# When GpSimd sums the squares of a norm in a three-block transformer kernel: behind the last remainder, or behind the split of the fourth weight tile

## The chip, the cores and the metric

The kernel is one program on one core of a Trainium2 chip. TensorE multiplies, VectorE and ScalarE work on elements, GpSimd adds squares and loads bias tables, SyncE issues the loads of the weights. The metric is the device time of one execution in microseconds, of which lower is better. The kernel before took 1948.46 us (median of three).

## The reference

The input x has 512 tokens of 1024 values. Three blocks follow each other: block A with windowed attention, block B with neighbourhood attention on a grid, and a third with dilated and stick-breaking attention. Each norm divides by a root of a mean of squares over the 1024 values of a token:

```python
def rms_norm(x, g):
    xf = x.astype(jnp.float32)
    y = xf * lax.rsqrt(jnp.mean(xf * xf, axis=-1, keepdims=True) + RMS_EPS)
    return (y * g.astype(jnp.float32)).astype(x.dtype)
```

In blocks A and B (i = 0 and 1) the part that matters here is

```python
        x = x + rms_norm(mixed, norm_mix_post[i])
        h = rms_norm(x, norm_ffn_pre[i])
        gu = jnp.einsum('bsd,df->bsf', h, w_gu[i])
        f = jnp.einsum('bsf,fd->bsd', jax.nn.silu(gu[..., :D_FF]) * gu[..., D_FF:], w_down[i])
        x = x + rms_norm(f, norm_ffn_post[i])
```

and then the next block's norm and its projection to queries, keys and values.

## The kernel before, in words

Activations lie with the feature on the partitions: x is `xT`, eight chunks of 128 features by 512 tokens. Each weight matrix is cut into tiles of 128 output features by 1024 input features. SyncE loads a tile into one of four slots of `w_raw`. ScalarE rounds it to `w_hi` (L566), VectorE subtracts to get the remainder `w_lo` (L982) and counts `w_split`. In the same way the activations are kept as `h_hi` (ScalarE, L609) and `h_lo` (VectorE, L1004, which counts `h_ready`). A product takes three matmuls for each chunk: `w_hi h_hi`, `w_hi h_lo`, `w_lo h_hi` (L1516 to L1518), so 24 matmuls of 512 columns for a tile.

The stages touched here are of the kind "stair": the two `gate_up` stages (44 tiles each), `proj[1]` (14 tiles) and `proj_dil` (12 tiles). Their tiles 0, 1 and 2 are multiplied together, chunk by chunk, as the chunks of the new x come out of the norm before (`stairs`, L1422 to L1430). From tile 3 on each tile is done in a whole. Before each tile TensorE waits for its `w_split`.

The norm that belongs to the stage doesn't hold the matmuls up. The gain is applied to h at once, and the factor for each token, `rstd`, is applied when a product's bank is read. So the mean of squares is made meanwhile: ScalarE squares the eight chunks into `sq_x` (L647), GpSimd adds them (`sum_kept`, L474, seven adds) and splits the sum into `sum_hi` and `sum_lo` (L480, L482), TensorE sums over the partitions with a matrix of minus ones (`add_all`, L1629 and L1630), and ScalarE takes a logarithm and an exponential (`statistic`, L618 and L621). These norms have the numbers 3 and 7 (for `gate_up`), 5 (for `proj[1]`) and 9 (for `proj_dil`).

Where TensorE makes the product over partitions is given by hand: `hooks` maps a place (tile, chunk) of the stage's order to a function that is called behind that chunk's three matmuls. `turn_rms` is a second hook: it waits for `rstd` and turns it into columns with matmuls of one column (L1639, L1641), for values that are read with tokens on the partitions.

The engines keep their own order. VectorE, in `dense`, splits tile k + 3 at step k and then reads the bank of tile k; eight tiles are split in front of step 0, so the first split in this loop is tile 8's, at step 5, behind the reads of tiles 0 to 4. ScalarE does the same with `w_hi`. In `gate_up` the reads (L1193) scale an even tile (gate) and an odd tile (up), ScalarE takes the Silu of the gate (L795), VectorE multiplies (L1198), ScalarE rounds (L798) and VectorE subtracts (L1200).

When GpSimd starts is a wait of its own:

```python
                pool.wait_ge(h_ready, DC * (4, 6)[layer] - 1)
                sum_kept(3 + 4 * layer, sq_x, S)
```

It starts at the seventh of the eight `h_lo` of this norm.

Of the kernel before, what the change touches and what calls it, by code (L numbers as in the profile page):

```python
# [11 lines left out]
DC = D // P  # L12
# [27 lines left out]
def program(nc, t, out):  # L40
# [25 lines left out]
    proj, mem_k, mem_v, v_in, w_out, gate_up, down = [], [], [], [], [], [], []  # L66
# [15 lines left out]
    proj_dil = Stage(tiles_of(t["w_qk_dil"], 12), stair=True)  # L82
# [13 lines left out]
    with ExitStack() as ctx:  # L96
# [76 lines left out]
        rstd = place("rstd", [P, S])  # L173
# [26 lines left out]
        ps = [ctx.enter_context(nc.psum_tensor(f"bank{i}", [P, 512], F32)) for i in range(8)]  # L200
# [6 lines left out]
        w_hi_done, w_split, unit_done = sem("w_hi_done"), sem("w_split"), sem("unit_done")  # L207
# [239 lines left out]
        def _(pool):  # L447
# [87 lines left out]
            for layer in range(2):  # L535
                if layer:
                    pool.dma_start(grid_masks[:, :], t["grid_masks"]).then_inc(masks_in, 16)
                    pool.wait_ge(masks_in, 16)
                biases(layer)
                sum_streamed(2 + 4 * layer)  # L540

                pool.wait_ge(h_ready, DC * (4, 6)[layer] - 1)
                sum_kept(3 + 4 * layer, sq_x, S)
                sum_streamed(4 + 4 * layer)
                pool.wait_ge(h_ready, DC * (5, 7)[layer] - 1)
                sum_kept(5 + 4 * layer, sq_x, S)
            biases(2)
            sum_streamed(10)
# [826 lines left out]
        def _(pe):  # L1375
# [115 lines left out]
            def dense(st, rhs, reads, wait_rhs=lambda chunk: None, hooks={}, begun=()):  # L1491

                begin_side()
                seen = 0
                if st.stair:
                    stairs(st, rhs, wait_rhs)
                for k, i, c in chunk_order(st):
                    if (k, c) in begun:  # L1500
                        continue
                    u, first, m = st.tiles[k][i]
                    if i == 0 and c == 0 and bank_before(st, k) >= 0:
                        s, n = reads(bank_before(st, k))
                        pe.wait_ge(s, n)
                    if c == 0:
                        pe.wait_ge(w_split, u + 1)
                    chunk = first + c
                    if k == 0:
                        wait_rhs(chunk)  # L1510
                    hi, lo = rhs(chunk) if st is not gates or k % 3 == 0 else (o2_hi[:, chunk, :], o2_lo[:, chunk, :])
                    acc = bank_of(st, side[0], k)[:, :st.width]
                    cols = slice(P * c, P * c + P)
                    w1, w2 = w_hi[:, u % 4, cols], w_lo[:, u % 4, cols]
                    start, end = i == 0 and c == 0, i == len(st.tiles[k]) - 1 and c == m - 1
                    mm(acc, w1, hi, start=start, stop=False)  # L1516
                    mm(acc, w1, lo, start=False, stop=False)  # L1517
                    last = mm(acc, w2, hi, start=False, stop=end)  # L1518
                    if c == m - 1:
                        last.then_inc(unit_done, 1)  # L1520
                    if (k, chunk) in hooks:
                        hooks[k, chunk]()
# [18 lines left out]
            def reads_of(sem_, base, counts=None):  # L1541
                return lambda k: (sem_, base + (k + 1 if counts is None else sum(counts[:k + 1])))
# [79 lines left out]
            def add_all(n, acc, width=S):  # L1622

                def add():
                    if n_norm[0]:
                        pe.wait_ge(ln_done, n_norm[0])
                    pe.wait_ge(masks_rounded, 3)
                    pe.wait_ge(sum_split, kept_stats.index(n) + 1)
                    mm(acc[:, :width], neg_ones[:, :], sum_hi[:, :width], start=True, stop=False)  # L1629
                    mm(acc[:, :width], neg_ones[:, :], sum_lo[:, :width], start=False, stop=True).then_inc(sq_summed, 1)  # L1630
                    n_norm[0] += 1
                return add

            def turn_rms(n, src, tiles, acc, first=0, classes=False):

                def turn():
                    pe.wait_ge(rstd_done, n + 1)
                    for r in range(4 if classes else 0):
                        mm(acc[:, 4 + r:5 + r], by_class(src[:, :])[:, r, :], ident[:, 0:1], start=True, stop=True)  # L1639
                    for kt in range(tiles):  # L1640
                        last = mm(acc[:, first + kt:first + kt + 1], src[:, P * kt:P * kt + P], ident[:, 0:1],  # L1641
                                  start=True, stop=True)
                    last.then_inc(col_ready, 1)
                    n_col[0] += 1
                return turn
# [153 lines left out]
            for layer in range(2):  # L1799
                n = 5 * layer  # L1800
                old = 4 * ((side[0] + 1) % 2)
                if layer == 0:
                    n_h[0] += DC

                counts = [1] * 6 + [4] * 2 + [1] * 2 if layer == 0 else [1] * 14

                def turn_both():
                    pe.wait_ge(rstd_done, 2)
                    pe.wait_ge(consts_in, 64)
                    turn_rms(0, rstd, 4, ps[old])()  # L1810
                    turn_rms(1, rstd_mem, 2, ps[old], 8)()

                if layer == 0:
                    hooks = {(3, 0): turn_table, (5, 2): add_first, (8, 3): add_all(1, ps[old], MEM), (9, 3): turn_both}
                else:
                    hooks = {(5, 2): add_all(n, ps[old]), (6, 3): turn_rms(n, rstd, 4, ps[old])}
                dense(proj[layer], h, reads_of(acc_read_dve, n_dve[0], counts), wait_h, hooks)
                end_side(dve=sum(counts), lent=sum(counts[:7]))
                if layer == 0:
                    n_h[0] += DC  # L1820
                    dense(mem_k[0], mh, None, wait_h)
                    end_side(dve=2)
                    values(mem_v[0], mh_hi, mh_lo, 2)
                if layer == 0:
                    values(v_in[0], h_hi, h_lo, 4)
                    n_h[0] += DC
                    dense(mem_k[1], mh, None, wait_h)
                    end_side(dve=2)
                    softmax(0, None, None, None, (mem_v[1][0], mh_hi, mh_lo, 2, 1), w_out[0])
                else:  # L1830
                    values_wide(v_in[1][0], h_hi, h_lo, 2)
                    softmax(1, None, None, None, (v_in[1][1], h_hi, h_lo, 4, 2), w_out[1])
                for inner in range(2):
                    n = 2 + 4 * layer + 2 * inner
                    new, old = 4 * (side[0] % 2), 4 * ((side[0] + 1) % 2)
                    if inner == 0:
                        def wait_o(c):
                            if c == DC - 1:
                                pe.wait_ge(o_ready, heads[0] - DC + c + 1)
                        dense(w_out[layer], h, reads_of(acc_read_act, n_act[0]), wait_o,  # L1840
                              {}, [(k, c) for k in range(2) for c in range(7)] + [(2, 0), (2, 1)])
                    else:
                        dense(down[layer], a, reads_of(acc_read_act, n_act[0]), wait_a(FC))
                    end_side(act=4)
                    after = (gate_up[layer], (proj[1], proj_dil)[layer])[inner].tiles[0][0][0]
                    wait_reads(freed[-2])
                    add_seven(n, ps[old + 3])()
                    add_last(n, ps[old + 3])
                    keep_busy(14, after)
                    n_x[0] += DC  # L1850
                    n_h[0] += DC
                    freed[-1] = (n_act[0], n_dve[0], n_x[0])
                    if inner:
                        continue
                    dense(gate_up[layer], h, reads_of(acc_read_dve, n_dve[0]), wait_h, {(5, 2): add_all(n + 1, ps[new])})
                    n_a[0] += FC
                    end_side(dve=2 * FC, lent=7)

            old = 4 * ((side[0] + 1) % 2)
            counts = [4] * 2 + [1] * 10  # L1860
            dense(proj_dil, h, reads_of(acc_read_dve, n_dve[0], counts), wait_h,
                  {(5, 2): add_all(9, ps[old]), (6, 3): turn_rms(9, rstd, 4, ps[old], 0, True)})
            end_side(dve=18, lent=13)
            values(v_dil[:1], h_hi, h_lo, 4)
            pe.wait_ge(hi_classed, DC)
# [245 lines left out]
```

## Time and profile before

| what | us |
|---|---|
| median of three runs | 1948.46 (1947.61 to 1950.47) |
| profiled execution, its own time | 1947.74 |
| its span, first to last instruction | 1945.9 |
| TensorE busy | 1927.0 |
| VectorE busy | 971.4 |
| ScalarE busy | 774.5 |
| GpSimd busy | 182.4 |

The span is covered by TensorE for 99%. Ends of matmuls are modelled and overlap the next start, so the distance between two starts says more than the duration. The profile names a line, an engine and the tiles written and read.

### The profile page before, as it was taken

What the parts mean: (1) busy time and instruction counts of PE and PEld (TensorE: products, weight loads), DVE (VectorE), ACT (ScalarE), POOL (GpSimd) and SP (SyncE); (2) the same over time, 40 slices, a digit from 0 to 9 for tenths busy, and PEclk for the clock granted to TensorE, in tenths of its full rate; (3) what the DMA queues carried; (4) which work ended last, traced back from release to release, by engine and by line L of the source; (5) the groups of instructions that cost most, each with busy time, mean ns of one, the idle gap of its engine ahead of it and who ended that gap; (6) DMA issues with size and microseconds to landing.
All of it is one profiled execution on the core that took longest, in us unless ns stands there. A gap on an engine that the chain in (4) does not pass through costs nothing.

```text
span 1945.9 us, 24129 instructions
## 1 busy us (share of the span) xinstructions
PE 1927.0 (99%) x9956; PEld 1568.2 (81%) x9956; DVE 971.4 (50%) x1464; ACT 774.5 (40%) x1252; POOL 182.4 (9%) x197
## 2 busy tenths in 40 slices
PE   9999999999999999999999999999999999999997
PEld 7967788888878867788888887878888888888886
DVE  5575665553227366565554227343665556425522
ACT  5386433333423176433333325233764443212321
POOL 4111300000105030210000003000000020000000
PEclk9999999999999999999999999999999999999999
DMA  6421223333333221233333333331212333322322
GB/s 192 142 60 44 86 90 97 96 97 100 92 101 99 94 64 34 80 99 93 97 97 98 94 101 108 98 109 44 77 30 87 111 98 98 98 95 94 96 96 85
DMA packets 52117, 178.72 MB, mean 92 GB/s; under 512 B 6380, under 2 KB 7788, under 8 KB 51880
## 3 DMA queue, kind: packets, MB, share of 16 engines
q1 hardware_dynamic: 49656, 169.14, 27.7%
q0 software_dynamic: 2208, 7.97, 1.5%
q8 instruction: 80, 1.31, 0.3%
q14 instruction: 29, 0.24, 0.0%
q10 hardware_dynamic: 144, 0.06, 0.0%
HBM read 174.48 MB, written 2.66 MB: 91 GB/s over the span
## 4 chain that ended last, share of the span: by engine, by line
PE 96%; DVE 2%; ACT 1%; issue 0%; DMA 0%; SPq 0%; DVEq 0%; ACTq 0%
PE bank L1516 24%; PE bank L1517 23%; PE bank L1518 23%; PE bank L1760 3%; PE bank L1717 2%; PE bank L1682 2%; PE bank L1535 2%; PE bank L1536 2%; PE bank L1537 2%; PE bank L1430 1%; PE bank L1422 1%; PE bank L1425 1%; PE bank L1574 1%; PE bank L1575 1%; PE bank L1576 1%; PE bank L1594 1%
## 5 line engine op out<-in xcount | busy, mean ns | idle before, releaser
L982 DVE TENSOR_TENSOR w_lo<-w_raw,w_hi 128x1024 fp32r<-128x1024 f32 (+2 forms) x325 | 403.9, 1244 | 733.9 <-ACT w_hi L566 733.4
L566 ACT CAST w_hi<-w_raw 128x1024 fp32r<-128x1024 f32 (+2 forms) x325 | 328.5, 1012 | 581.3 <-DMA w_raw<-in_w_down 133.7
L1516 PE MATMUL bank<-h_hi,w_hi 128*128 128x512 f32 x1288 | 503.0, 391 | 0.2 <-DVE q_buf L1048 0.2
L1517 PE MATMUL bank<-h_lo,w_hi 128*128 128x512 f32 x1288 | 501.8, 390 | 0.0
L1518 PE MATMUL bank<-h_hi,w_lo 128*128 128x512 f32 x1288 | 501.8, 390 | 0.0
L1516 PE MATMUL bank<-a_hi,w_hi 128*128 128x512 f32 (+1 forms) x752 | 289.4, 385 | 0.0
L1517 PE MATMUL bank<-a_lo,w_hi 128*128 128x512 f32 (+1 forms) x752 | 289.2, 385 | 0.0
L1518 PE MATMUL bank<-a_hi,w_lo 128*128 128x512 f32 (+1 forms) x752 | 289.1, 384 | 0.0
L1516 PEld LDWEIGHTS bank<-h_hi,w_hi 128*128 128x128 f32 x1288 | 242.0, 188 | 53.4 <-DVE w_lo L982 1.6
L1518 PEld LDWEIGHTS bank<-h_hi,w_lo 128*128 128x128 f32 x1288 | 242.2, 188 | 50.8
L1517 PEld LDWEIGHTS bank<-h_lo,w_hi 128*128 128x128 f32 x1288 | 242.2, 188 | 49.8
L1516 PEld LDWEIGHTS bank<-a_hi,w_hi 128*128 128x128 f32 x752 | 141.3, 188 | 28.3 <-DVE a_lo L1312 0.3
L1518 PEld LDWEIGHTS bank<-a_hi,w_lo 128*128 128x128 f32 x752 | 141.3, 188 | 28.2
L1517 PEld LDWEIGHTS bank<-a_lo,w_hi 128*128 128x128 f32 x752 | 141.3, 188 | 28.1
L460 POOL COPY sq_sum<-sq 128x512 f32<-128x512 f32 x6 | 3.7, 624 | 1061.1 <-ACT sq L605 1061.1
L693 ACT ACTIVATE prob_short<-prob_short,low_stat 128x256 f32<-128x256 f32 (+6 forms) x144 | 74.7, 525 | 19.8 <-DVE low_stat L1093 19.8
L463 POOL TENSOR_TENSOR sq_sum<-sq_sum,sq 128x512 f32<-128x512 f32 x37 | 51.7, 1397 | 283.0 <-ACT sq L605 283.0
L798 ACT CAST a_hi<-raw 128x512 fp32r<-128x512 f32 x44 | 27.3, 621 | 125.4 <-DVE raw L1198 125.4
L795 ACT ACTIVATE act_out<-act_out 128x512 f32<-128x512 f32 x44 | 27.8, 632 | 95.1 <-DVE act_out L1193 95.0
L1682 PEld LDWEIGHTS bank<-ident,prob_short 128*128 128x128 f32 (+3 forms) x340 | 36.0, 138 | 25.6 <-DVE prob_short L1115 19.7
L1682 PE MATMUL bank<-ident,prob_short 128*128 128x128 f32 (+3 forms) x340 | 53.4, 284 | 1.4 <-DVE prob_short L1115 1.0
L1535 PE MATMUL bank<-h_hi,w_hi 128*128 128x512 f32 x128 | 52.5, 410 | 1.8 <-ACT v_buf L777 1.8
(232 smaller groups left out, 2313.4 us busy)
## 6 DMA issues: line engine op xcount, KB each, us to landing
w_raw<-in_w_gu SPq DMA_DIRECT2D x88, 512.0 KB, 3.5
w_raw<-in_w_mlp_in SPq DMA_DIRECT2D x32, 512.0 KB, 3.5
w_raw<-in_w_mlp_out SPq DMA_DIRECT2D x32, 512.0 KB, 3.5
w_raw<-in_w_down SPq DMA_DIRECT2D x32, 448.0 KB, 3.3
w_raw<-in_w_out SPq DMA_DIRECT2D x24, 512.0 KB, 3.6
w_raw<-in_w_down SPq DMA_DIRECT2D x16, 512.0 KB, 3.6
w_raw<-in_w_gates SPq DMA_DIRECT2D x16, 512.0 KB, 3.5
w_raw<-in_w_qk_b SPq DMA_DIRECT2D x14, 512.0 KB, 3.6
```

The lines of the kernel that those rows point to most:

```text
L463: made = nc.gpsimd.tensor_tensor(sq_sum[:, :], sq_sum[:, :], sq[:, c % 2, :], ALU.add)
L566: nc.scalar.copy(slot(w_hi, v), slot(w_raw, v)).then_inc(w_hi_done, 1)
L693: nc.scalar.activation(part, part, ACT.Exp, bias=top, scale=-1.0, accum_out=sums[:, s % 4, half, k:k + 1]).then_inc(p_exp, 1)
L982: nc.vector.tensor_tensor(slot(w_lo, v), slot(w_raw, v), slot(w_hi, v).bitcast(F32), ALU.subtract).then_inc(w_split, 1)
L1516: mm(acc, w1, hi, start=start, stop=False)
L1517: mm(acc, w1, lo, start=False, stop=False)
L1518: last = mm(acc, w2, hi, start=False, stop=end)
L1535: mm(ps[7][:, :], w1, hi, start=c == 0, stop=False)
L1536: mm(ps[7][:, :], w1, lo, start=False, stop=False)
L1537: last = mm(ps[7][:, :], w2, hi, start=False, stop=c == DC - 1)
L1682: last = nc.tensor.transpose(bank_in(phase, 4 + turned[0] % 2)[:w, base + P * kt:base + P * kt + P], prob_of(phase, d, half)[:, at_ + firs ...
L1760: last = mm(out_, v, turned_p, start=x == 0, stop=x == n_v - 1, skip_group_check=phase == 2)
```

## The change

GpSimd waits for the split of the stage's fourth weight tile (tile 3) in place of the seventh remainder of h. TensorE's product over partitions moves from behind tile 5, chunk 2 to behind tile 6, chunk 0, and the turning of rstd from behind tile 6, chunk 3 to behind tile 6, chunk 4.

```diff
-                pool.wait_ge(h_ready, DC * (4, 6)[layer] - 1)
+                pool.wait_ge(w_split, gate_up[layer].tiles[3][0][0] + 1)
                 sum_kept(3 + 4 * layer, sq_x, S)
                 sum_streamed(4 + 4 * layer)
-                pool.wait_ge(h_ready, DC * (5, 7)[layer] - 1)
+                pool.wait_ge(w_split, (proj[1], proj_dil)[layer].tiles[3][0][0] + 1)
                 sum_kept(5 + 4 * layer, sq_x, S)
...
-                    hooks = {(5, 2): add_all(n, ps[old]), (6, 3): turn_rms(n, rstd, 4, ps[old])}
+                    hooks = {(6, 0): add_all(n, ps[old]), (6, 4): turn_rms(n, rstd, 4, ps[old])}
...
-                    dense(gate_up[layer], h, reads_of(acc_read_dve, n_dve[0]), wait_h, {(5, 2): add_all(n + 1, ps[new])})
+                    dense(gate_up[layer], h, reads_of(acc_read_dve, n_dve[0]), wait_h, {(6, 0): add_all(n + 1, ps[new])})
...
-                  {(5, 2): add_all(9, ps[old]), (6, 3): turn_rms(9, rstd, 4, ps[old], 0, True)})
+                  {(6, 0): add_all(9, ps[old]), (6, 4): turn_rms(9, rstd, 4, ps[old], 0, True)})
```

The first norm of the kernel (number 0) and the memory's (number 1) keep their waits and places.

## Rows read from the trace of the kernel before

**Rows 1.** The page's chain that ended last, share of the span by engine.

```profile
PE 96%; DVE 2%; ACT 1%; issue 0%; DMA 0%; SPq 0%; DVEq 0%; ACTq 0%
```

**Rows 2.** What TensorE's weight loads waited for: us in total, times, longest.

```profile
PEld bank L1516 <- DVE w_lo L982: 1.6, 5, 0.3
```

**Rows 3.** GpSimd in order of time, norm 3: start, duration, instruction, idle time before.

```profile
230.57 1.29 POOL L474 TENSOR_TENSOR sq_sum<-sq_x 128x512 f32<-128x512 f32 x1 [22.35 <-DVE h_lo L1004]
232.00 11.12 POOL L474 TENSOR_TENSOR sq_sum<-sq_sum,sq_x 128x512 f32<-128x512 f32 x6
...
244.76 1.29 POOL L482 TENSOR_TENSOR sum_lo<-sq_sum,sum_hi 128x512 fp32r<-128x512 f32 x1
```

**Rows 4.** VectorE in order of time, the same stretch and on to tile 10.

```profile
230.62 1.79 DVE L1004 SCALAR_TENSOR_TENSOR h_lo<-xT,gains,h_hi 128x512 fp32r<-128x512 f32 x1
232.33 2.30 DVE L982 TENSOR_TENSOR w_lo<-w_raw,w_hi 128x1024 fp32r<-128x1024 f32 x1
...
237.97 1.77 DVE L982 TENSOR_TENSOR w_lo<-w_raw,w_hi 128x1024 fp32r<-128x1024 f32 x1 [3.33 <-ACT w_hi L566]
...
249.80 1.13 DVE L1193 TENSOR_TENSOR act_out<-bank,rstd 128x512 f32<-128x512 f32 x1 [2.67 <-ACT rstd L621]
...
260.85 1.23 DVE L982 TENSOR_TENSOR w_lo<-w_raw,w_hi 128x1024 fp32r<-128x1024 f32 x1 [1.64 <-ACT w_hi L566]
...
269.38 1.22 DVE L982 TENSOR_TENSOR w_lo<-w_raw,w_hi 128x1024 fp32r<-128x1024 f32 x1 [1.64 <-ACT w_hi L566]
```

**Rows 5.** TensorE in order of time: starts of tiles 3, 4, 8, and the product.

```profile
234.43 0.39 PE L1430 MATMUL bank<-h_lo,w_hi 128*128 128x512 f32 x1
234.69 0.50 PE L1516 MATMUL bank<-h_hi,w_hi 128*128 128x512 f32 x1
...
240.27 0.39 PE L1516 MATMUL bank<-h_hi,w_hi 128*128 128x512 f32 x1
...
247.75 0.40 PE L1629 MATMUL bank<-sum_hi,neg_ones 128*128 128x512 f32 x1
...
262.52 0.39 PE L1516 MATMUL bank<-h_hi,w_hi 128*128 128x512 f32 x1
```

**Rows 6.** ScalarE in order of time, from rstd to the rounding of tile 8.

```profile
249.78 1.28 ACT L849 ACT_TABLE_LOAD   x1
...
259.25 0.63 ACT L795 ACTIVATE act_out<-act_out 128x512 f32<-128x512 f32 x1 [1.80 <-DVE act_out L1193]
259.78 1.03 ACT L566 CAST w_hi<-w_raw 128x1024 fp32r<-128x1024 f32 x1
```

**Rows 7.** Layer 1's gate_up (norm 7), TensorE and VectorE in order of time.

```profile
836.76 0.40 PE L1629 MATMUL bank<-sum_hi,neg_ones 128*128 128x512 f32 x1
...
849.64 1.23 DVE L982 TENSOR_TENSOR w_lo<-w_raw,w_hi 128x1024 fp32r<-128x1024 f32 x1 [1.64 <-ACT w_hi L566]
...
851.54 0.39 PE L1516 MATMUL bank<-h_hi,w_hi 128*128 128x512 f32 x1
```

**Rows 8.** Projection of block B (norm 5), TensorE, ScalarE and VectorE in order of time.

```profile
614.33 0.40 PE L1629 MATMUL bank<-sum_hi,neg_ones 128*128 128x512 f32 x1
...
615.72 0.63 ACT L621 ACTIVATE rstd<-rstd 128x512 f32<-128x512 f32 x1
...
619.38 1.22 DVE L982 TENSOR_TENSOR w_lo<-w_raw,w_hi 128x1024 fp32r<-128x1024 f32 x1
...
630.06 0.39 PE L1516 MATMUL bank<-h_hi,w_hi 128*128 128x512 f32 x1
```

**Rows 9.** TensorE's turning of norm 9, the stretch with its clock (PEclk, third from the end), and one stand-still.

```profile
1209.94 1.80 PE L1639 MATMUL bank<-ident,rstd 128*128 128x1 f32 x8
...
1213.80:1217.30 3.50, 3.50 (x10) 2.72 (x9) 2.15 (x4) 0.00 (x0) 0.00 (x0) 0.51 0.00 0
...
1280.10 0.50 PE L1535 MATMUL bank<-h_hi,w_hi 128*128 128x512 f32 x1 [1.80 <-ACT v_buf L777]
```

## The prediction

> **What bounds the kernel.** I first read the share of the chain that ended last: 96% of it is TensorE [rows 1]. The reader should take from this that only two things count: time in which TensorE stands still, and time in which its clock is low. The second view is what TensorE's weight loads waited for. The wait that the change aims at is there, and it is small: five waits of L1516 for VectorE's w_lo, 1.6 us together, none over 0.3 us [rows 2]. Then I read the four engines in order of time around the first feed-forward norm. In it seven squared chunks are added by GpSimd, from 230.57 to 246.05 us, 15.5 us in all [rows 3]. In this stretch VectorE's subtraction of a weight tile takes 2.30 and 1.77 us, where one with GpSimd at rest takes 1.23 us (the one at 260.85), and the last h_lo takes 1.79 us [rows 4]. Tile 3 (the fourth) is split at 232.33 + 2.30 = 234.63 us and TensorE starts it at 234.69, 0.26 us after the matmul in front of it [rows 4, 5]. The pitch of the stream is (247.75 - 240.27) / 33 = 0.227 us (tile 4's 24 matmuls and three chunks of tile 5), so this start is 0.03 us late, and the first matmul takes 0.50 us and not 0.39, another 0.11 [rows 5].
>
> **What the first edit gives.** The sums now start when tile 3 is split. The two operations of VectorE in front of that point (h_lo, w_lo) lose their company: the split ends some 2 us earlier, near 232.3 us, and TensorE no longer waits. That removes 0.03 + 0.11 = 0.14 us here. The same place occurs four times (norms 3, 5, 7 and 9), and the five waits of rows 2 are no larger elsewhere, so I count 4 x 0.15 = 0.6 us. Both ends: nothing (tile 4's split takes the place of tile 3's) and 1.6 us, all of the waits in rows 2. Tile 4 is split at 237.97 + 1.77 = 239.74 and wanted at 240.27 [rows 4, 5]. Its split starts when its w_hi is there, which the edit leaves alone, and runs beside GpSimd before and after. Even at 2.30 us it ends at 240.27, just about in time, so I keep the 0.6.
>
> The adds move from 230.57 to about 232.3 us. With the same company they would take the same 15.5 us, to 247.8 us. GpSimd's later work (the masks and bias tables of the next attention, the next streamed sum) moves by the same 1.8 us and is wanted only behind the whole projection or feed-forward stage that has just begun, which covers it. SyncE's queue isn't touched, and no DMA of GpSimd is on TensorE's way.
>
> The page SBUF — State Buffer of the Trainium skill, section Who interferes with whom, says that a VectorE instruction with two SBUF inputs and a GpSimd instruction that reads SBUF exclude each other on a shared port, and that who comes first blocks the other for the whole instruction. The 2.30 us against 1.23 agree with that. By this rule the change moves the contention rather than removing it: the splits of tiles 4 to 7 are still beside the adds. Were tile 4's blocked for a whole add, 1.29 us by its row, it would end at 237.97 + 1.23 + 1.29 = 240.49 and take 0.3 us back at each place. The sum would be 0.6 us instead of a gain.
>
> **What the second edit costs.** The product over partitions (L1629, L1630) stands behind tile 5's chunk 2 now, at 247.75 us [rows 5], and GpSimd's last operation ends at 246.05 [rows 3]: 1.7 us to spare. New place: behind tile 6's chunk 0, six chunks of three matmuls later, 18 x 0.227 = 4.08 us. There the sum has about 4 us to spare, so the product doesn't wait for GpSimd. But everything behind the product is 4.08 us later as well. In order: ScalarE makes rstd, loads the Silu table from 249.78 on, and VectorE begins at 249.80 to read the banks [rows 4, 6]. Then the two engines hand each other every pair: read, read, Silu, product, round, remainder. The code puts the w_hi and w_lo of tile 8 behind the read and Silu of tile 4. So ScalarE rounds tile 8 at 259.78, directly behind the Silu of 259.25 and with no wait for its DMA [rows 6], VectorE subtracts from 260.85 to 262.08 [rows 4], and TensorE starts tile 8 at 262.52 [rows 5]. The margin is 0.44 us, of which 0.06 is the hand-over seen at tile 3: 0.38 us. I find no wait in this chain for anything but its own members, from 249.78 to 262.08, so it moves as one piece. TensorE will then stand still for 4.08 - 0.38 = 3.70 us before tile 8 of layer 0. Layer 1 repeats it: product at 836.76, tile 8 split at 849.64 + 1.23 = 850.87, wanted at 851.54, margin 0.67 - 0.06 = 0.61 [rows 7], a stop of 3.47 us. With 0.11 for each restart: 3.70 + 3.47 + 0.22 = 7.4 us. Tile 9 and those behind it don't stop again: two tiles further the split stands at 269.38, so a tile costs the pair of engines (269.38 - 260.85) / 2 = 4.27 us [rows 4] and TensorE 24 x 0.227 = 5.44 us; the engines run ahead from there.
>
> **The two projections** (norms 5 and 9) move too, but their readers only scale: VectorE has read five tiles and splits tile 8 from 619.38 to 620.60, and TensorE wants it at 630.06 [rows 8]. 4.08 us later is still 5.4 us early. The turning of rstd moves by one chunk only, from (6, 3) to (6, 4). From the product's start at 614.33 to the end of rstd at 615.72 + 0.63 = 616.35 are 2.02 us [rows 8], and the new distance is 0.46 + 12 x 0.227 = 3.18 us. It waits for nothing, 1.16 us to spare. The dilated projection repeats this pattern, with copies for the classes between the reads on the same two engines. I cost both at nothing. The cover is TensorE's own work on tiles 6 and 7; if it were gone, each would cost up to 4.08 us, as above.
>
> **The clock.** TensorE's granted clock is 1.00 of full speed (2.4 GHz) nearly throughout. It fell once, to 0.51 (1.2 GHz) from 1213.80 to 1217.30, behind a stretch of 16 matmuls of one column that began at 1209.94 (eight of them in 1.80 us). Behind a stand-still of 1.80 us at 1280.10 it did not fall [rows 9]. The stop that I expect, some 3.6 us, is longer than both. A fall costs half of 3.5 us at most, 1.75 us for each stop, and nothing at least. Part of the low time may fall into the stop itself, so I take 1.2 us each, 2.4 us in all.
>
> The page TensorE: Matmul & The Clock Gate of the Trainium skill, section What's actually happening, says that the half rate is the resting state and that activity releases it. The one fall in this trace agrees. By that rule both stops are followed by a low stretch; if it were wrong for them, the sum would be the one of the second rival.
>
> **Sum.** -0.6 + 7.4 + 0 + 2.4 = +9.2 us. The profiled execution took 1947.74 us (span 1945.9 and 1.8 around it), which is 0.7 us below the median of the runs shown, 1948.46. So 1956.9 by the one and 1957.7 by the other; I say 1957.4.
>
> **The rivals.**
> - The edits cancel or gain (the other side, 2% for a gain over 0.2%, 7% for within 0.2%). Mechanism: the reads in the Silu chain get shorter once they no longer follow the busy stretch, so that tile 8 is split early enough. The bound of 0.2% is 3.9 us; with the 0.6 gained, the two stops with all they bring must stay under 4.5 us, so the chain of 12.3 us would have to give back over 1.4 us in each layer. Against it: GpSimd is already at rest from 246.05 us, so nothing relieves the reads. If the stops halved, the time would be 1948.5 + 3.7 - 0.6 = 1951.6 with no fall of the clock; without any stop, 1947.9. For a gain over 0.2% TensorE would need 3.9 us back, and the waits on w_lo are 1.6 us in all.
> - The stops come and the clock stays up (20%): 7.4 - 0.6 = +6.8, 1955.3. For it: the 1.80 us stop did not lower the clock. Against it: the stop is twice as long.
> - The stops come with the whole low stretch, or a projection loses time as well (16%): 7.4 - 0.6 + 3.5 = +10.3, 1958.8; one projection's wait at the (6, 4) hook would add a microsecond or two, to 1960.5.
> - The change does nothing since GpSimd isn't where the split is slow (contained in the first rival): the rows of GpSimd and VectorE overlap exactly, and the moved product still costs.
>
> **Numbers.** My forecast (both stops, the clock low behind them for part of it) has 55%. Range 1953.5 to 1960.3: it holds the forecast, the rival without the clock and most of the third. About 0.2% (3.9 us) is what a measurement of this kernel can tell from no change. Slower by more than that: 0.91; within: 0.07; faster: 0.02.
>
> **What would show it.** In the changed profile: tile 3's split at about 1.2 us with the wait of L1516 gone; the first L474 add behind it; the product at about 251.7 us; one wait of TensorE on w_lo (L982) of 3.4 to 3.8 us near 262.4 and one near 851.4 us; a granted clock of 0.5 for some 3.5 us behind them; the chain from rstd to tile 8's split still 12.3 us long; no new wait at the turning of rstd. I am wrong if tile 8's w_lo ends before TensorE is through tile 7, or if the product waits for sum_lo at its new place.

## The result, and the profile after

The changed kernel took 1958.12 us (median of five, 1956.4 to 1960.69) against 1948.46: 9.7 us more, ratio 1.0049 with a 95% interval of 1.0038 to 1.0061. The forecast was 1957.4. The profiled execution took 1957.06 us, its span is 1955.2 us, 9.3 more than the span before. Below, the rows of the profile after are set against those of before.

What TensorE's matmuls waited for (us in total, times, longest) has a new first row. Before, waits for w_lo stood at the weight loads alone, 1.6 us in all [rows 2]:

```profile
PE bank L1516 <- DVE w_lo L982: 7.4, 3, 3.6
```

GpSimd in order of time, norm 3:

```profile
232.97 1.28 POOL L474 TENSOR_TENSOR sq_sum<-sq_x 128x512 f32<-128x512 f32 x1 [24.36 <-DVE w_lo L982]
...
246.91 1.29 POOL L482 TENSOR_TENSOR sum_lo<-sq_sum,sum_hi 128x512 fp32r<-128x512 f32 x1
```

VectorE in order of time, from the last h_lo to tile 8's split:

```profile
231.00 0.75 DVE L1004 SCALAR_TENSOR_TENSOR h_lo<-xT,gains,h_hi 128x512 fp32r<-128x512 f32 x1
231.67 1.22 DVE L982 TENSOR_TENSOR w_lo<-w_raw,w_hi 128x1024 fp32r<-128x1024 f32 x1
238.30 5.81 DVE L982 TENSOR_TENSOR w_lo<-w_raw,w_hi 128x1024 fp32r<-128x1024 f32 x3 [5.41 <-ACT w_hi L566]
...
254.04 1.13 DVE L1193 TENSOR_TENSOR act_out<-bank,rstd 128x512 f32<-128x512 f32 x1 [7.68 <-ACT rstd L621]
...
265.04 1.23 DVE L982 TENSOR_TENSOR w_lo<-w_raw,w_hi 128x1024 fp32r<-128x1024 f32 x1 [1.63 <-ACT w_hi L566]
```

TensorE in order of time: the start of tile 3, the product, the last matmul of tile 7 and the first of tile 8:

```profile
234.76 0.39 PE L1430 MATMUL bank<-h_lo,w_hi 128*128 128x512 f32 x1
234.99 0.39 PE L1516 MATMUL bank<-h_hi,w_hi 128*128 128x512 f32 x1
...
251.99 0.40 PE L1629 MATMUL bank<-sum_hi,neg_ones 128*128 128x512 f32 x1
...
262.45 0.39 PE L1518 MATMUL bank<-h_hi,w_lo 128*128 128x512 f32 x1
266.41 0.47 PE L1516 MATMUL bank<-h_hi,w_hi 128*128 128x512 f32 x1 [3.57 <-DVE w_lo L982]
266.72 0.39 PE L1517 MATMUL bank<-h_lo,w_hi 128*128 128x512 f32 x1
```

The first edit does what it says: the last h_lo takes 0.75 us (before 1.79), tile 3's split 1.22 (before 2.30), TensorE starts tile 3 in step, 0.23 us behind its predecessor, and its first matmul takes 0.39 us and not 0.50 [rows 4, 5]. The sum is whole at 246.91 + 1.29 = 248.20, 3.8 us ahead of the product at 251.99. The second edit costs what the forecast's chain said: from 254.02 (the table load on ScalarE) to 265.04 + 1.23 = 266.27 is still 12.25 us (12.30 before), and tile 8 starts at 266.41, where TensorE was through with tile 7's matmuls at 262.45 + 0.23 = 262.68. It stands still for 3.73 us.

Layer 1, TensorE and VectorE, and then the stretches behind both stops (busy time by engine; the granted clock, as a share of full speed, is third from the end):

```profile
854.72 0.39 PE L1518 MATMUL bank<-h_hi,w_lo 128*128 128x512 f32 x1
...
857.07 1.23 DVE L982 TENSOR_TENSOR w_lo<-w_raw,w_hi 128x1024 fp32r<-128x1024 f32 x1 [1.63 <-ACT w_hi L566]
...
858.44 0.57 PE L1516 MATMUL bank<-h_hi,w_hi 128*128 128x512 f32 x1 [3.33 <-DVE w_lo L982]
```

```profile
266.50:270.00 3.50, 3.50 (x16) 2.87 (x17) 2.52 (x4) 1.58 (x2) 0.00 (x0) 1.00 0.00 0
...
858.70:862.10 3.40, 3.40 (x9) 2.62 (x9) 2.43 (x4) 1.56 (x2) 0.00 (x0) 0.50 0.00 0
```

A stop of 3.49 us, and behind this one the clock at 0.50 of full speed (1.2 GHz) for 3.4 us; behind the first one it stayed at 1.00. So the two stops are the same in kind and length, and one of them cost 1.7 us more.

Laid side by side by the number of the matmul, the two traces drift apart at these places: +3.85 us at tile 8 of layer 0; +3.5 at tile 8 of layer 1 and +1.7 in the matmuls at the low clock behind it; about -0.2 around each of the four starts of tile 3, -0.8 in all; and +0.8 at tile 4 of norm 9, once, of which more below. That is about +9.0. The rest is some tenths either way, of which +0.4 from the first ten microseconds of the kernel, where the two executions already differ.

In the projection of block B the turning of rstd stands where it was forecast, without a wait:

```profile
622.20 0.40 PE L1629 MATMUL bank<-sum_hi,neg_ones 128*128 128x512 f32 x1
...
623.59 0.63 ACT L621 ACTIVATE rstd<-rstd 128x512 f32<-128x512 f32 x1
...
625.41 0.95 PE L1641 MATMUL bank<-ident,rstd 128*128 128x1 f32 x8
```

### The profile page after: what moved, and what is told of

It reads as the page before. It is cut to its first block, busy times and chain, and to the rows that moved or that the text cites. A ratio compares the mean times of both kernels' runs of the same rounds, so it can differ in the third digit from the quotient of the medians.

```text
span 1955.2 us, 24129 instructions
## 1 busy us (share of the span) xinstructions
PE 1928.9 (99%) x9956; PEld 1569.5 (80%) x9956; DVE 959.5 (49%) x1464; ACT 774.1 (40%) x1252; POOL 180.8 (9%) x197
## 4 chain that ended last, share of the span: by engine, by line
PE 95%; DVE 3%; ACT 1%; DMA 1%; issue 0%; SPq 0%; DVEq 0%; ACTq 0%
PE bank L1516 23%; PE bank L1517 23%; PE bank L1518 23%; PE bank L1760 3%; PE bank L1717 2%; PE bank L1682 2%; PE bank L1535 2%; PE bank L1536 1%; PE bank L1537 1%; PE bank L1430 1%; PE bank L1422 1%; PE bank L1425 1%; PE bank L1574 1%; PE bank L1575 1%; PE bank L1576 1%; PE bank L1595 1%
## 5 line engine op out<-in xcount | busy, mean ns | idle before, releaser
L982 DVE TENSOR_TENSOR w_lo<-w_raw,w_hi 128x1024 fp32r<-128x1024 f32 (+2 forms) x325 | 396.2, 1221 | 736.0 <-ACT w_hi L566 735.6
L1516 PE MATMUL bank<-h_hi,w_hi 128*128 128x512 f32 x1288 | 503.4, 391 | 7.6 <-DVE w_lo L982 7.4
L1193 DVE TENSOR_TENSOR act_out<-bank,rstd 128x512 f32<-128x512 f32 x44 | 48.4, 1101 | 15.5 <-ACT rstd L621 15.4
```

The source lines that it names most:

```text
L982: nc.vector.tensor_tensor(slot(w_lo, v), slot(w_raw, v), slot(w_hi, v).bitcast(F32), ALU.subtract).then_inc(w_split, 1)
L1193: nc.vector.tensor_tensor(dst, of, reordered(layer, raw[:, p, :], rstd[:, :])[1], ALU.mult).then_inc(acc_read_dve, 1)
```

## The experiments

Each was timed against the kernel before on its own chip, whose medians lay between 1948.35 and 1949.08 us; differences are against that median. Edits are shown against the changed kernel, so in the first two a plus line puts the old state back.

### The second edit alone

```diff
-                pool.wait_ge(w_split, gate_up[layer].tiles[3][0][0] + 1)
+                pool.wait_ge(h_ready, DC * (4, 6)[layer] - 1)
...
-                pool.wait_ge(w_split, (proj[1], proj_dil)[layer].tiles[3][0][0] + 1)
+                pool.wait_ge(h_ready, DC * (5, 7)[layer] - 1)
```

> The second edit alone: the product over partitions behind tile 6, chunk 0 and the turning behind tile 6, chunk 4, GpSimd's sums where they were before. Theory (the chain from rstd to tile 8's split moves by 4.08 us): two stops of TensorE before tile 8 of gate_up, 3.7 and 3.5 us, the four starts of tile 3 as slow as before, a clock fall behind none to two of the stops; 1957 to 1960 us, some 0.6 us more than the change. Rival (GpSimd's later start is what costs): near 1949 us.

1960.12 us, +11.0, ratio 1.0058 (1.0045 to 1.0070), at the upper edge of what was expected. The two waits on w_lo are 6.9 us together, as in the change. The loss is the second edit's. In this profile the clock fell behind the stop of layer 0 and not behind that of layer 1.

### The first edit alone

```diff
-                    hooks = {(6, 0): add_all(n, ps[old]), (6, 4): turn_rms(n, rstd, 4, ps[old])}
+                    hooks = {(5, 2): add_all(n, ps[old]), (6, 3): turn_rms(n, rstd, 4, ps[old])}
...
-                    dense(gate_up[layer], h, reads_of(acc_read_dve, n_dve[0]), wait_h, {(6, 0): add_all(n + 1, ps[new])})
+                    dense(gate_up[layer], h, reads_of(acc_read_dve, n_dve[0]), wait_h, {(5, 2): add_all(n + 1, ps[new])})
...
-                  {(6, 0): add_all(9, ps[old]), (6, 4): turn_rms(9, rstd, 4, ps[old], 0, True)})
+                  {(5, 2): add_all(9, ps[old]), (6, 3): turn_rms(9, rstd, 4, ps[old], 0, True)})
```

> The first edit alone: GpSimd waits for the split of tile 3, the product stays behind tile 5, chunk 2. Theory: the four waits for tile 3's split are gone (0.6 us gained), and the product now waits 0.3 to 0.5 us for sum_lo at each of four places, and as much of tile 8's margin of 0.38 us in gate_up is eaten; no stop before tile 8 above 0.3 us; 1948.5 to 1950.5 us. Rival (GpSimd's later start is what costs): most of the change's 9.7 us, near 1957 us.

1948.96 us, -0.1 by the medians, ratio 1.0006 (0.9997 to 1.0015): no change, or a loss of at most 2.9 us. The four waits for tile 3's split are gone. What the weight loads and then the matmuls waited for:

```profile
PEld bank L1516 <- DVE w_lo L982: 0.3, 1, 0.3
...
PE bank L1629 <- POOL sum_lo L482: 1.4, 4, 0.6
```

The product's four waits take more than the starts of tile 3 gave back. Laid beside the profile before, TensorE loses 0.4 to 0.8 us at each product, 2.3 us in all, and gains 0.8 us at the four starts. The timed runs can't tell this net loss of 1.5 us from nothing.

Tile 8 of layer 0 is split at 261.80 + 1.23 = 263.03 us here and TensorE takes it up at 263.47, so the margin there is still 0.44 us. I had expected it to be eaten, and it was not: the product's wait delays TensorE as much as it delays rstd.

### Tile 8 rounded and split ahead of rstd

```diff
-                hi_to(split + 4)
+                hi_to(split + (4 if inner else 5))
...
-                lo_to(w_out[layer].after(DC - 1) + 7)
+                lo_to(w_out[layer].after(DC - 1) + 8)
```

> The whole change, and in the two gate_up stages ScalarE rounds and VectorE subtracts tile 8 before they come to rstd and the reads (its load is there, as tile 4 is through). Theory: both stops before tile 8 go; tile 9's split, still behind the reads, may be up to 0.4 us late; no clock fall but the one behind the turning; 1948 to 1950 us. Rival (the clock or the adds beside the splits of tiles 4 to 7 make the loss): no lower than 1955 us.

1947.82 us, -1.3, ratio 0.9995 (0.9987 to 1.0004), a little under what was expected: the whole loss of 9.7 us goes with the order of one rounding and one subtraction in each layer. Nothing else of the change is touched; the product stands at its late place and VectorE begins its reads as late as in the change. VectorE and then TensorE in order of time:

```profile
251.09 1.23 DVE L982 TENSOR_TENSOR w_lo<-w_raw,w_hi 128x1024 fp32r<-128x1024 f32 x1 [4.40 <-ACT w_hi L566]
254.35 1.14 DVE L1193 TENSOR_TENSOR act_out<-bank,rstd 128x512 f32<-128x512 f32 x1 [2.04 <-ACT rstd L621]
...
267.17 1.23 DVE L982 TENSOR_TENSOR w_lo<-w_raw,w_hi 128x1024 fp32r<-128x1024 f32 x1 [0.26 <-ACT w_hi L566]
```

```profile
262.99 0.39 PE L1516 MATMUL bank<-h_hi,w_hi 128*128 128x512 f32 x1
...
268.21 0.39 PE L1518 MATMUL bank<-h_hi,w_lo 128*128 128x512 f32 x1
268.55 0.47 PE L1516 MATMUL bank<-h_hi,w_hi 128*128 128x512 f32 x1
```

Tile 8 starts in step at 262.99. Tile 9 is the next to be late, by 0.1 us, since its split is still behind the reads.

### The change in the projections only

```diff
-                pool.wait_ge(w_split, gate_up[layer].tiles[3][0][0] + 1)
+                pool.wait_ge(h_ready, DC * (4, 6)[layer] - 1)
...
-                    dense(gate_up[layer], h, reads_of(acc_read_dve, n_dve[0]), wait_h, {(6, 0): add_all(n + 1, ps[new])})
+                    dense(gate_up[layer], h, reads_of(acc_read_dve, n_dve[0]), wait_h, {(5, 2): add_all(n + 1, ps[new])})
```

> The change in the two projections only, the two gate_up stages as before (wait and place). Theory: the projections cost nothing but what tile 4's split of norm 9 may be late; -0.3 for the two tile 3 starts, +0.7 for that one if it comes again; 1948 to 1949.5 us. Rival (the turning of rstd or the projections' reads have a part in it): 1951 us or more.

1947.12 us, -2.0 by the medians, ratio 0.9995 (0.9986 to 1.0004), 0.9 us under what was expected. The clock fell nowhere between the first matmuls and the last in this profile. The projections cost nothing, as they were priced; a gain of 0.3 us is below what this can tell.

### A smaller and a larger delay in gate_up

The product behind tile 5, chunk 5 (2.04 us later than before) and behind tile 6, chunk 4 (6.8 us later):

```diff
-                    dense(gate_up[layer], h, reads_of(acc_read_dve, n_dve[0]), wait_h, {(6, 0): add_all(n + 1, ps[new])})
+                    dense(gate_up[layer], h, reads_of(acc_read_dve, n_dve[0]), wait_h, {(5, 5): add_all(n + 1, ps[new])})
```

> The whole change, but in gate_up the product stands behind tile 5, chunk 5: three chunks, 2.04 us, later than before and not six. Theory (the delay of the product less the margin): stops of 2.04 - 0.38 = 1.7 and 1.4 us before tile 8, short enough to leave the clock up mostly; 1951 to 1953.5 us. Rival (any stop before tile 8 costs the whole, or the loss isn't in proportion): 1955 us or more, or under 1950 us.

> The whole change, but in gate_up the product stands behind tile 6, chunk 4: ten chunks, 6.8 us, later than before. Theory: 6.8 - 0.38 = 6.4 and 6.2 us of stops in each gate_up, in one piece or with a first part before tile 7, whose bank is tile 0's; 5.4 us over the change, and both clock falls, 1963 to 1966.5 us. Rival (the loss has come to its end with the change): 1958 us.

1950.69 us (+1.7, ratio 1.0012, 1.0003 to 1.0021; 0.3 us under what was expected) and 1963.98 us (+15.0, ratio 1.0080, 1.0067 to 1.0094; as expected). What TensorE waited for in the one and the other:

```profile
PE bank L1516 <- DVE w_lo L982: 3.0, 2, 1.6
```

```profile
PE bank L1516 <- DVE w_lo L982: 10.7, 2, 5.4
...
PE bank L1516 <- DVE act_out L1193: 1.0, 2, 0.5
```

The waits follow the delay: 3.0 us for 2.04, 6.9 for 4.08 and 11.7 for 6.8 (two layers each). The last has a first part of 0.5 us before tile 7, for its bank, as expected. Twice the delay less the two margins (0.38 + 0.61) would be 3.1, 7.2 and 12.6; this view counts a wait from the modelled end of the matmul before, 0.16 us behind the start that the next could have had, which is most of the difference. With the larger delay the clock was low for 6.8 us around the end of each long stop; in layer 0 from 268.1 us on, and the stop ended at 269.33, so that the first 1.2 us of it cost nothing.

### TensorE kept at work through the stops

```diff
+                    def fill():
+                        pe.wait_ge(ln_done, n_norm[0])
+                        for _ in range(15):
+                            mm(ps[4 * ((side[0] + 1) % 2)][:, :], neg_ones[:, :], h_hi[:, 0, :], start=True, stop=True)
+
-                    dense(gate_up[layer], h, reads_of(acc_read_dve, n_dve[0]), wait_h, {(6, 0): add_all(n + 1, ps[new])})
+                    dense(gate_up[layer], h, reads_of(acc_read_dve, n_dve[0]), wait_h, {(6, 0): add_all(n + 1, ps[new]), (7, DC - 1): fill})
```

> The whole change, and 15 matmuls of 512 columns (15 x 0.227 = 3.4 us) into a free bank between tile 7 and tile 8 of both gate_up stages: TensorE works through the stops and is no earlier at tile 8. Theory that the stops cost 7.4 us and the clock falls behind them the rest: no fall behind either stop, the start of tile 8 where it was, 1955 to 1957 us, 1 to 3 us under the change. Rival (the clock has no share that counts): the change's 1958 us.

1954.51 us, +5.6, ratio 1.0032 (1.0020 to 1.0045). The start of tile 8 is where it was:

```profile
262.59 3.66 PE L1858 MATMUL bank<-h_hi,neg_ones 128*128 128x512 f32 x15
266.47 0.47 PE L1516 MATMUL bank<-h_hi,w_hi 128*128 128x512 f32 x1 [0.21 <-DVE w_lo L982]
```

TensorE's clock is 1.00 behind both. The time is 0.5 us under what was expected, and 4.1 us lower than the change came out against its own base. So both were run again side by side on one chip:

> The changed kernel as it is, on one chip with the next. Theory: 8.5 to 11 us over the kernel before, the stops of 3.7 and 3.5 us in the profile, and a clock fall behind at least one of them in most executions.

> The changed kernel with the 15 matmuls in both stops. Theory: what the stops cost in time stays (+7.2 us less the 0.6 us of tile 3), and the fall of the clock behind them goes, 1.7 us for each that came; 2 to 3.4 us under the changed kernel beside it. Rival (the stops cost more than their length for another reason): under 1 us between the two.

1956.05 us (+7.7, ratio 1.0040, 1.0027 to 1.0052) and 1955.24 us (+6.9, ratio 1.0037, 1.0023 to 1.0051). The change came out under the 8.5 us that were expected of it. The two are 0.8 us apart, and under 1 us was what the expectation had named for its rival, that the stops cost more than their length for another reason than the clock. So by the medians this pair speaks against the clock and the first pair for it, and the intervals of the second pair overlap widely.

Two other records decide. The first are the profiles. In the three executions with stops of 3.5 and 3.7 us (the change, the change again, the second edit alone) the clock fell behind four of six stops, each time for 3.4 us and 1.7 us of loss: behind both in the change again, behind one in each of the others. In the two with the filler it fell behind none of four.

The second is the mean granted clock that is on record for every timed execution. A span of 1955.2 us with a mean clock of 0.996 lacks 0.4% of it, 7.8 us, to full speed: that is what the low clock took away, at most (a low stretch behind the last matmul costs nothing and is in it for every kernel). This number is 5.8 us on average in the 58 executions of the kernel before that were timed with these experiments, 7.8 us in the ten of the change (both sets) and 5.1 us in the eleven with the filler. So the low clock takes 2.0 us more in the change than before (standard error 0.9), and 2.7 us more than with the filler (standard error 1.1). What is left, the span times the clock, is 6.6 us longer in the change than before, and 7.2 us with the filler (standard error 0.4 each). These are rough, as the clock is on record to three digits, and 0.001 of it is 2 us; but they have the sign and the size of the first record.

The stretches behind both stops of the change's second profile:

```profile
267.20:270.60 3.40, 3.40 (x10) 2.63 (x9) 2.43 (x4) 1.56 (x2) 0.00 (x0) 0.50 0.00 0
861.10:864.50 3.40, 3.40 (x10) 2.63 (x9) 2.46 (x4) 1.56 (x2) 0.00 (x0) 0.50 0.00 0
```

### A kernel with both gains

The change with tile 8 split early as above, the product behind tile 5, chunk 4 in all four stages, and the turning behind tile 6, chunk 3 in the two projections.

```diff
-                hi_to(split + 4)
+                hi_to(split + (4 if inner else 5))
...
-                lo_to(w_out[layer].after(DC - 1) + 7)
+                lo_to(w_out[layer].after(DC - 1) + 8)
...
-                    hooks = {(6, 0): add_all(n, ps[old]), (6, 4): turn_rms(n, rstd, 4, ps[old])}
+                    hooks = {(5, 4): add_all(n, ps[old]), (6, 3): turn_rms(n, rstd, 4, ps[old])}
...
-                    dense(gate_up[layer], h, reads_of(acc_read_dve, n_dve[0]), wait_h, {(6, 0): add_all(n + 1, ps[new])})
+                    dense(gate_up[layer], h, reads_of(acc_read_dve, n_dve[0]), wait_h, {(5, 4): add_all(n + 1, ps[new])})
...
-                  {(6, 0): add_all(9, ps[old]), (6, 4): turn_rms(9, rstd, 4, ps[old], 0, True)})
+                  {(5, 4): add_all(9, ps[old]), (6, 3): turn_rms(9, rstd, 4, ps[old], 0, True)})
```

> The first edit, the product behind tile 5, chunk 4 (turning behind tile 6, chunk 3), and tile 8 rounded and split before rstd in gate_up. Theory: GpSimd's sum is just there, no wait for tile 3's split, nothing late at tile 8: the 0.6 us of the four starts are kept and no more; 1947.5 to 1949 us, the same as before within its noise. Rival (the product waits for sum_lo here too, or tile 9 is late): 1949.5 us or more.

1947.91 us, -1.1, ratio 0.9995 (0.9986 to 1.0003). No matmul of TensorE waits for w_lo or sum_lo. It can't be told from the kernel before: the 0.8 us or so around the starts of tile 3 are all that there was to win.

## Why the prediction was right

**What the first edit gives.** Forecast 0.6 us, 0.15 at each of four places; in all nine profiles with the first edit in all four stages the stretch around each start of tile 3 is 0.2 us shorter, 0.8 us in all. The forecast counted the late start and its longer first matmul; the last matmuls in front of it came a little earlier too, by 0.08 us in norm 3. In the first edit alone the product spends the gain again, and more; together with the second it is kept.

**What the second edit costs.** Forecast stops of 3.70 and 3.47 us; the profile has 3.73 and 3.49. The early split (loss gone), the delays of three, six and ten chunks (loss in proportion) and the second edit alone (loss as before) show that it is this chain. The adds' later start and their company have no part in it that could be measured: in the early split they are as late as in the change, and the loss is gone; in the first edit alone they cost 2.9 us at most.

**The two projections.** Forecast nothing; with them alone changed no cost was found, and the turning had 625.41 - (623.59 + 0.63) = 1.19 us to spare against 1.16 forecast.

**The clock.** Forecast 1.2 us for each stop, chosen between nothing and 1.75; found 1.7 us behind four of six stops, 1.1 us on average. By the clocks of the timed executions it is 2.0 us for both stops together, where the forecast had 2.4, and 6.6 us for the rest, where it had 7.4 - 0.6 = 6.8. So both terms were right in kind and about right in size. The upper bound held for stops of this length only: with the stops of 5.4 and 5.6 us of the largest delay a low stretch was 6.8 us long.

**What of it is luck.** That the time came within 0.7 us of the forecast is in part chance. The same kernel, run again, came out 7.7 us and not 9.7 us over the kernel before. And the profile reaches its +9.3 with other terms than the sum: one fall of the clock and not a part of two, and 0.8 us at tile 4 of norm 9, which the forecast had at nothing.

**The contention, by the Trainium skill's rule of exclusion** (SBUF — State Buffer, Who interferes with whom). The change moved it to later splits, as the rule would have it: the first split beside the adds in norm 9 took 2.32 us. The forecast held that even 2.30 us would be just in time, and that a split blocked for a whole add would take the gain back. No matmul waited for tile 4's split in any profile but one, so the gain was not taken back. In that one, the change's first, ScalarE had tile 4 late (its load landed later: w_hi began 1201.45 - 1198.83 = 2.62 us after the start of tile 3, against 1192.53 - 1190.26 = 2.27 before), and TensorE stood for half a microsecond and lost 0.8 us with the restart. It took both: a split of 1.23 us would have ended at 1203.77, before TensorE was through with tile 3. ScalarE, VectorE and TensorE in order of time:

```profile
1201.45 1.05 ACT L566 CAST w_hi<-w_raw 128x1024 fp32r<-128x1024 f32 x1 [6.16 <-DMA w_raw<-in_w_qk_dil]
...
1202.54 2.32 DVE L982 TENSOR_TENSOR w_lo<-w_raw,w_hi 128x1024 fp32r<-128x1024 f32 x1 [5.85 <-ACT w_hi L566]
...
1204.91 0.50 PE L1516 MATMUL bank<-h_hi,w_hi 128*128 128x512 f32 x1 [0.49 <-DVE w_lo L982]
```

So this third wait for w_lo, which the forecast had at nothing, exists, but it came in one profile of the ten that have the first edit at norm 9, and it is not why the kernel got slower. Why this load landed later stays open.

## What to carry to other kernels

Before an operation is moved to "where there is time", follow its result through the queues of the engines that read it and look for other work that stands behind those reads: here a weight tile's split, wanted 0.44 us after it was done, and nothing to do with the norm. The price of a delay is the delay less that margin, once for each place, and it can be read from two rows of the trace; here some 2 us came on top for the low clock behind the stops. And where work that depends on nothing late stands behind work that does, put it in front: two changed counts took the whole loss away.

## What the runs showed that was not expected

The stand-still of 1.80 us at 1280.10, which the forecast used as a case where the clock stays up [rows 9], is followed by a low clock in other executions. In the first edit alone it ends at 1282.03, and behind it:

```profile
1282.80:1286.20 3.40, 3.40 (x9) 2.67 (x8) 1.22 (x1) 1.08 (x2) 0.00 (x0) 0.50 0.01 2
```

The same place and the turning of norm 9 were followed by a low stretch in some profiles and not in others, with the same instructions: of the twelve profiles of this study three had a low stretch behind neither place and three behind both. In one more (the kernel with both gains) the stretch behind the turning was 6.8 us long. A low stretch of 3.4 us costs 1.7 us, so two executions of one kernel can differ by 3.4 us for this alone, close to the 0.2% that a measurement here can tell. The timed executions of the kernel before agree: the six with a mean clock of 0.999 took 1946.4 us on average, the 23 with 0.996 took 1949.7 us.
